# One 128x128 transpose per step in place of eight 64x64 passes, in the triangular inverses of a hybrid mixer kernel

## What is computed

```python
def step(state, inp):
    r_t, w_t, k_t, v_t, kk_t, a_t = inp
    sk = jnp.einsum('bhij,bhj->bhi', state, kk_t)
    state = (state * w_t[:, :, None, :]
             - sk[..., None] * (kk_t * a_t)[:, :, None, :]
             + v_t[..., None] * k_t[:, :, None, :])
    return state, jnp.einsum('bhij,bhj->bhi', state, r_t)
...
_, o = lax.scan(step, s0, xs)
```

## Time and profile before

| | us |
|---|---|
| median of 3 timed runs | 955.85 |
| lowest, highest | 953.41, 956.14 |
| the profiled execution | 953.54 |
| its span from first to last instruction | 951.7 |
| loop of the inverses in it, first L757 to the first L610 behind | 124.02 to 143.63 |

### The profile page before, as it was taken

One profiled execution on the slowest core, in us unless ns is written; L12 is line 12 of the kernel. 1 busy time (PEld: TensorE's weight loads), 2 busy tenths in 40 slices (PEclk: granted clock), 3 DMA queues, 4 the chain that ended last, 5 costly groups with the idle time before them and its releaser, 6 DMA issues.

```text
span 951.7 us, 21560 instructions
## 1 busy us (share of the span) xinstructions
PE 941.5 (99%) x7320; PEld 915.1 (96%) x7320; DVE 748.3 (79%) x1618; ACT 616.7 (65%) x1219; POOL 645.4 (68%) x324
## 2 busy tenths in 40 slices
PE   8999999999999999999999999999999999999997
PEld 7998899999889999999999999999999999999996
DVE  7683574634665889888788888769999999999996
ACT  6874367555557676676899999865555555555553
POOL 4686634488325999999988889966566566567640
PEclk9999999999999999999999999999999999999999
DMA  7463312355654766666555566679999999999981
GB/s 267 145 233 133 133 49 90 110 179 180 223 195 134 250 225 216 217 218 215 199 180 180 182 206 229 217 267 411 408 394 379 403 387 377 408 389 386 386 324 45
DMA packets 67043, 232.36 MB, mean 244 GB/s; under 512 B 8211, under 2 KB 10259, under 8 KB 66860
## 3 DMA queue, kind: packets, MB, share of 16 engines
q1 hardware_dynamic: 52588, 180.51, 53.1%
q0 software_dynamic: 13824, 50.34, 14.0%
q10 hardware_dynamic: 576, 0.82, 0.2%
HBM read 229.67 MB, written 1.06 MB: 242 GB/s over the span
## 4 chain that ended last, share of the span: by engine, by line
PE 97%; DVE 1%; DMA 1%; ACT 0%; issue 0%; ACTq 0%; POOL 0%; DVEq 0%
PE PS L976 21%; PE PS L1047 20%; PE PS L980 12%; PE PS L1051 12%; PE PS L922 3%; PE PS L610 3%; PE PS L614 3%; PE PS L611 3%; PE PS L542 2%; PE PS L534 2%; PE PS L533 2%; PE PS L532 2%; PE PS L933 2%; PE PS L1001 1%; PE PS L1002 1%; PE PS L707 1%
## 5 line engine op out<-in xcount | busy, mean ns | idle before, releaser
L1579 POOL TENSOR_TENSOR lo<-raw,hi 128x1024 fp32r<-128x1024 f32 x191 | 456.7, 2411 | 133.7 <-ACT hi L1129 121.0
L1129 ACT CAST hi<-raw 128x1024 fp32r<-128x1024 f32 x203 | 212.5, 1048 | 56.1 <-DMA raw<-in_u_units 36.6
L976 PE MATMUL PS<-xb,hi 128*128 128x416 f32 x1024 | 219.4, 356 | 0.0
L1047 PE MATMUL PS<-xb,hi 128*128 128x416 f32 x1008 | 213.4, 352 | 0.0
L976 PEld LDWEIGHTS PS<-xb,hi 128*128 128x128 f32 x1024 | 182.5, 189 | 0.9
L1047 PEld LDWEIGHTS PS<-xb,hi 128*128 128x128 f32 x1008 | 179.1, 189 | 1.0
L2274 DVE TENSOR_TENSOR lo<-raw,hi 128x2048 fp32r<-128x2048 f32 x63 | 144.2, 2288 | 7.8 <-ACT hi L1469 7.5
L1469 ACT CAST hi<-raw 128x1024 fp32r<-128x1024 f32 x128 | 134.1, 1047 | 2.4 <-DMA raw<-in_v_units 2.2
L980 PEld LDWEIGHTS PS<-xb,lo 128*128 128x128 f32 x1024 | 133.5, 191 | 1.1 <-POOL lo L1579 0.6
L980 PE MATMUL PS<-xb,lo 128*128 128x208 f32 x1024 | 133.6, 273 | 0.0
L1051 PEld LDWEIGHTS PS<-xb,lo 128*128 128x128 f32 x1008 | 132.4, 191 | 0.7 <-DVE lo L2274 0.5
(11 more groups left out here) (367 smaller groups left out, 1578.4 us busy)
## 6 DMA issues: line engine op xcount, KB each, us to landing
raw<-in_u_units SPq DMA_DIRECT2D x128, 512.0 KB, 3.3
raw<-in_v_units SPq DMA_DIRECT2D x128, 512.0 KB, 6.8
raw<-in_w_in_units SPq DMA_DIRECT2D x43, 512.0 KB, 3.3
raw<-in_w_q_units SPq DMA_DIRECT2D x16, 512.0 KB, 3.2
raw<-in_w_proj_units SPq DMA_DIRECT2D x8, 512.0 KB, 3.3
raw<-in_w_out_units SPq DMA_DIRECT2D x8, 512.0 KB, 3.3
arena<-bias_rows SPq DMA_DIRECT2D x2, 512.0 KB, 5.8
arena<-in_subkeys_t SPq DMA_DIRECT2D x1, 1024.0 KB, 5.5
```

Source lines behind the costliest of these rows:

```text
L976: mm(o[:, 0:2 * TD], hi[:, w, P * k:P * k + P], joined[:, k, 0:2 * TD], start=(k == 0), stop=False, skip_group_check=True)
L1047: return mm(PS[:, V_BANKS[c], 0:2 * TD], hi[:, (U_V + j) % 4, P * c:P * c + P], coef_slot(u + j)[:, 0:2 * TD], start=start, stop=False, sk ...
L1129: nc.scalar.copy(hi[:, j, :], raw[:, j, :]).then_inc(hi_made, 1)
L1579: nc.gpsimd.tensor_tensor(lo[:, w, :], raw[:, w, :], hi[:, w, :].bitcast(F32), ALU.subtract).then_inc(lo_pool, 1)
```

## The change

- **The turn.** In steps 0 to 19 `flip(s)` is one transpose of 128x128 with the whole identity instead of four 64x64 matmuls. It turns the two slots (64 columns each) and both halves at once, so in `W8` the slot is now on the partitions and the half along the free axis. Steps 20 to 23 stay as they were.
- **The first product.** With `W8` laid out so, two of its four 64x64 blocks need the left factor on the other 64 partitions. These crossed factors are made once: two 64x64-weight matmuls of 256 columns with the identity move them into bank 1, behind the scores and ahead of `value_unit(29)`; ScalarE copies them to `S8_crossed`; GpSimd makes `S32_crossed` from that by one masked multiply of 128x256, ahead of its copy of step 4. The four matmuls now use all four quarters of the array, and the rows' halves write two different banks.
- **Banks.** The three products of a step use banks 2q and 2q+1, all eight in all. So the loop starts only when the values are copied out (`vA_sb`), and `flip(1)` waits for the copy of unit 30 (bank 0). `units(31)` waits for `changed(20)` (`x_sb` at 21). Masks and copies read the first product from two banks.
- **The exponentials.** ScalarE's list has two of them ahead of the value copies and three behind, then `gate_copy(30)`; the eight of 256 columns stand at odd steps 1 to 15, the last three of 128 at steps 2, 6 and 10.

```diff
+        def level_at(s):
+            return 2 * (s % 4) + 1 if s < STEPS - 4 else (1, 0, 5, 7)[s % 4]
+        def level_bank(s):
+            return PS[:, level_at(s), 0:P].rearrange("p (a b) -> p a b", b=HD)
+        def p1_banks(s):
+            return PS[:, 2 * (s % 4):2 * (s % 4) + 2, 0:HD] if s < STEPS - 4 else level_bank(s)
...
+            for d in range(2):
+                last = mm(PS[half_rows(1 - d), 1, 0:4 * HD], ident[half_rows(d), half_rows(d)], S8[half_rows(d), 1 - d::2, :],
+                          start=True, stop=True)
+            last.then_inc(sides_ps, 1)
             value_unit(29)
...
             def flip(s):
                 if s >= 4:
                     pe.wait_ge(x_sb, s - 3)
+                if s < STEPS - 4:
+                    nc.tensor.transpose(PS[:, level_at(s), 0:P], WT[:, pairs(s % 4), :].rearrange("p a b -> p (a b)"), ident
+                                        ).then_inc(flip_ps, 1)
+                    return
...
             def first_product(s):
                 pe.wait_ge(flip_sb, s + 1)
-                for m, rows, side in level_blocks(s):
-                    across = mats[rows, 8 * (m // 4) + 4 * (1 - side) + m % 4, 2, half_rows(side)]
-                    inputs = across if s >= STEPS - 4 else (S32 if s >= STEPS - 8 else S8)[rows, m, :]
-                    last = mm(level_out(s, m, side), inputs, W8[rows, m, :], start=True, stop=True)
+                if s < STEPS - 4:
+                    q, wide = s % 4, s >= STEPS - 8
+                    if wide:
+                        pe.wait_ge(sides_sb, 2)
+                    for e, d in ((0, 0), (1, 1), (0, 1), (1, 0)):
+                        if e == d:
+                            left = (S32 if wide else S8)[half_rows(e), 2 * q + e, :]
+                        else:
+                            left = (S32_crossed if wide else S8_crossed)[half_rows(e), q, :]
+                        last = mm(p1_banks(s)[half_rows(d), e, :], left, W8[half_rows(e), 2 * q + d, :], start=True, stop=True)
...
-            pe.wait_ge(xt_dve, 1)
+            pe.wait_ge(sides_sb, 1)
+            pe.wait_ge(vA_sb, 2)
             pe.wait_ge(sc_sb, HEADS)
             for s in range(STEPS):
+                if s == 1:
+                    pe.wait_ge(act_evac, copied(30))
...
+                pe.wait_ge(x_sb, STEPS - 3)
                 units(31 + 3 * n)
...
+                    if lv == 1 and q == 0:
+                        pool.wait_ge(sides_sb, 1)
+                        nc.gpsimd.tensor_tensor(S32_crossed, S8_crossed, con[:, C_NM1 + 3 * HD:C_NM1 + 4 * HD].unsqueeze(1)
+                                                .to_broadcast([P, 4, HD]), ALU.mult).then_inc(sides_sb, 1)
```

More of the change, by code:

```diff
@@ L232, in block_program @@
         nSK = area(R0 + 23040, 1024, 2, 512)
+        S8_crossed, S32_crossed = area(R0 + 23040, 256, 4, HD), area(R0 + 23296, 256, 4, HD)
         ST = area(R0 + 24064, 512, 2, CT, HD)
@@ L748, in level_out @@
             def level_out(s, m, d):
-                return PS[half_rows(d), 4 + s % 4, HD * (m % 2):HD * (m % 2) + HD]
+                return PS[half_rows(d), level_at(s), HD * (m % 2):HD * (m % 2) + HD]
             def flip(s):
@@ L763, in first_product @@
                 pe.wait_ge(flip_sb, s + 1)
-                for m, rows, side in level_blocks(s):
-                    across = mats[rows, 8 * (m // 4) + 4 * (1 - side) + m % 4, 2, half_rows(side)]
-                    inputs = across if s >= STEPS - 4 else (S32 if s >= STEPS - 8 else S8)[rows, m, :]
-                    last = mm(level_out(s, m, side), inputs, W8[rows, m, :], start=True, stop=True)
+                if s < STEPS - 4:
[8 more added lines that the diff above has]
+                        last = mm(p1_banks(s)[half_rows(d), e, :], left, W8[half_rows(e), 2 * q + d, :], start=True, stop=True)
+                else:
+                    for m, rows, side in level_blocks(s):
+                        across = mats[rows, 8 * (m // 4) + 4 * (1 - side) + m % 4, 2, half_rows(side)]
+                        last = mm(level_out(s, m, side), across, W8[rows, m, :], start=True, stop=True)
                 last.then_inc(p1_ps, 1)
@@ L1284, in _ @@
                 hi_ahead(g, 0, 0)
-            act.wait_ge(unit_done, 30)
-            for n in range(NT):
-                nc.scalar.copy(vtokA[:, n, :], PS[:, 2 + n, :]).then_inc(vA_sb, 1)
+            act.wait_ge(sides_ps, 1)
+            nc.scalar.copy(S8_crossed.rearrange("p j t -> p (j t)"), PS[:, 1, 0:4 * HD]).then_inc(sides_sb, 1)
             def exponential(h, n):
@@ L1293, in exponential @@
                                      accum_out=small[:, 16 + 8 * n + h:17 + 8 * n + h]).then_inc(sc_exp, 1)
+            for h in range(2):
+                exponential(h, 0)
+            act.wait_ge(unit_done, 30)
+            for n in range(NT):
+                nc.scalar.copy(vtokA[:, n, :], PS[:, 2 + n, :]).then_inc(vA_sb, 1)
             def first_copied(s):
                 act.wait_ge(p1_ps, s + 1)
-                nc.scalar.copy(P1[:, pairs(s % 4), :], level_bank(s % 4)).then_inc(p1_act, 1)
-            for h in range(4):
+                nc.scalar.copy(P1[:, pairs(s % 4), :], p1_banks(s)).then_inc(p1_act, 1)
+            for h in range(2, 5):
                 exponential(h, 0)
+            gate_copy(30)
             for s in range(STEPS):
                 act.wait_ge(flip_ps, s + 1)
-                nc.scalar.copy(W8[:, pairs(s % 4), :], level_bank(s % 4)).then_inc(flip_sb, 1)
+                nc.scalar.copy(W8[:, pairs(s % 4), :], level_bank(s)).then_inc(flip_sb, 1)
                 if s > STEPS - 8:
                     first_copied(s - 1)
[L1307 to L1312, removed]
+                elif s % 2:
+                    exponential(s // 2, 1)
+                elif s in (2, 6, 10):
+                    exponential(5 + s // 4, 0)
             first_copied(STEPS - 1)
@@ L1888, in masked @@
                 across = con[:, C_LV + HD * lv:C_LV + HD * lv + HD].unsqueeze(1).to_broadcast([P, 2, HD])
-                V.tensor_tensor(P1[:, pairs(q), :], level_bank(q), across, ALU.mult).then_inc(p1_sb, 1)
+                V.tensor_tensor(P1[:, pairs(q), :], p1_banks(s), across, ALU.mult).then_inc(p1_sb, 1)
             def changed(s):
@@ L1895, in changed @@
                 dve.wait_ge(kept, columns_kept(s))
-                w, change = WT[:, pairs(q), :], level_bank(q)
+                w, change = WT[:, pairs(q), :], level_bank(s)
                 old, new = VT[lv % 2][:, pairs(q), :], VT[(lv + 1) % 2][:, pairs(q), :]
```

8 lines of the change are left out of this document (3 added, 5 removed).

## The result

| | before | after |
|---|---|---|
| median of 20 timed runs each, us | 955.39 | 956.52 |
| lowest, highest | 953.41, 956.72 | 955.02, 958.27 |
| the profiled execution | 953.54 | 956.57 |

The ratio of after to before is 1.0013 (95% interval 1.0007 to 1.0019): 1.1 to 1.2 us slower, against a forecast of +1.1. The change is real by this interval and too small to matter: far inside the 0.3% that the prediction called no change.

The account below looks back on a forecast made before the run. TensorE's list was taken to bound the kernel. The terms, 0.63 - 2.5 - 2.3 + 5.3 + 0.1 - 0.1 = +1.1 us, put on the median of 955.85, gave 957.0 us, range 953.0 to 960.5.

Parts of the forecast that it names:

- (a): Ahead of value_unit(29), two matmuls moving the crossed factors add 0.63 us to TensorE's list; bounds 0.48 and 1.1.
- (b): In the loop, 20 turns fall from 0.233 to 0.109 us each: -2.5 us.
- (c): In the loop, 20 first products on four quarters take 0.117 us in place of 0.233: -2.3 us.
- rival A: In the loop, the first product does not run four at a time; at 0.233 us, 959.3 us; chance 0.16.
- (d): In steps 2 to 19, changes of tiling around each transpose cost 0.293 us a step: +5.3 us.
- rival B: In the loop, a lone transpose costs no change of tiling: -1.8 us, 954.1 us; chance 0.22.
- (e): At the loop's start, flip(1) waits for unit 30's copy, with the first W copy queued behind: +0.1 us.
- (f): Around the loop, GpSimd's 0.6 us multiply, two-bank masks, ScalarE's exponentials and unit 31's wait cost nothing.
- (g): In steps 20 to 23, unchanged, changed(16) comes a little earlier against flip(20): -0.1 us.
- Rival C: In the loop, TensorE's clock falls from 2.4 to 1.2 GHz, giving near 967 us; chance 0.03.

Follow-up runs that it names:

- second_turn_beside: The changed kernel with an extra unused transpose right ahead of the turn in steps 1 to 19; ratio 1.0026 to the kernel before.
- second_turn_apart: The changed kernel with an extra unused transpose between first and second product in steps 1 to 19; ratio 1.0078 to the kernel before, four runs.
- sides_only: The kernel before with the two matmuls that move the crossed factors added, their result unused; ratio 0.9997 to the kernel before.
- crossing_by_dma: The changed kernel with the crossed factors moved by two DMAs instead of two matmuls and a copy; ratio 1.0009 to the kernel before.
- pairs: The changed kernel with steps taken in pairs on TensorE, halving the changes of tiling; ratio 1.0020 to the kernel before.
- pairs_dma: The changed kernel with steps in pairs and the crossed factors moved by two DMAs; ratio 1.0012 to the kernel before.
- quarter_turns: The changed kernel with turns 0 to 19 as four 64x64 matmuls on the array's four quarters; ratio 0.9997 to the kernel before.
- quarter_turns_dma: The changed kernel with turns on four quarters, crossed factors by DMA and turn 0 in free banks; 953.70 us, ratio 0.9983 to the kernel before.
- quarter_turns_dma_dense: As quarter_turns_dma, with an exponential in each of steps 1 to 11 of ScalarE's list; ratio 0.9992 to the kernel before.
- dense_exponentials: The changed kernel with an exponential in each of steps 1 to 11 of ScalarE's list; 955.98 us in one execution.

## Why the prediction held

**The bound.** TensorE's list set the end: 1.12 us of it in the trace became 1.13 between the medians. That these agree to 0.01 is luck, for the interval of the ratio is 0.7 to 1.8 us. What carries the claim is all the kernels together. The middle column is what the trace adds to TensorE's list, the moves and the stretch from unit 30 to unit 31; the last is the ratio in us:

| kernel | list, us | time, us |
|---|---|---|
| after | +1.12 | +1.2 (0.7 to 1.8) |
| `second_turn_beside` | +2.99 | +2.5 (1.4 to 3.5) |
| `second_turn_apart` | +8.52 | +7.4 (5.9 to 9.0) |
| `sides_only` | +0.58 | -0.3 (-1.1 to 0.6) |
| `crossing_by_dma` | +0.54 | +0.9 (-0.1 to 1.8) |
| `pairs` | +1.28 | +1.9 (1.0 to 2.8) |
| `pairs_dma` | +0.70 | +1.1 (0.3 to 2.1) |
| `quarter_turns` | +0.60 | -0.3 (-1.1 to 0.6) |
| `quarter_turns_dma` | -1.57 | -1.6 (-2.6 to -0.8) |
| `quarter_turns_dma_dense` | -0.99 | -0.8 (-1.7 to 0.1) |

All lie within their intervals, `sides_only` and `quarter_turns` at the very end of theirs.

**(a), the moves, +0.63**: 0.58, in two kernels. The four passes do overlap, by the price of the two score passes above, though the two row halves write one bank. The 1.1 by the rule of the Trainium skill ("TensorEngine Tiling (Array Packing)", Restrictions and Gotchas, Gotcha 1) did not come about; these halves write different partitions of the bank, and that they overlap there is all that the rows show.

**(b), the turns**: the extra transpose beside the turn added 0.11; 0.109 was forecast.

**(c), the first products**: the second product starts 0.165 behind the first, at most 0.05 of it the dearer first pass behind a change; so the eight passes take the 0.117 that was forecast, not the 0.233 of rival A. `quarter_turns_dma` has the same group without a change beside it, at 0.12.

**(d), the changes**: 0.31 for a visit, 0.293 forecast. The extra transpose apart tests this term almost by itself (tiling and kind of instruction, as said there), and it is the one that decides the case: rival B, that it is nothing, would have made the kernel faster. The split was off where the sum was not. I had put the next turn 0.38 behind the second product; it came 0.33 behind, and the 0.05 sits in the first product, the first group behind the change. The step came out at 0.753 where 0.75 was forecast.

**(e), the start, +0.1**: here errors cancelled. From the first turn to the first product it is +0.07 (125.21 to 126.09 for 124.02 to 124.83). The sum had -0.15 there, because (b) took 0.25 off for turns 0 and 1, which the wait for the copy of unit 30 covers, as (e) itself says. Against this 0.22 stand 0.09 that turn 0 no longer pays for a change of tiling, left out of the sum, and 0.06 in the groups up to turn 3. From unit 30 to turn 3 the terms of the sum come to -0.07 (three turns, two first products, three visits and this 0.1), and the trace has 0.

**(f), at nothing**: GpSimd's multiply is 0.7 long, not 0.6, and hidden; the masks of two banks cost no more (0.20 from the mask to the next operation, where it was 0.24); the looser ScalarE was worth nothing, as `dense_exponentials` says.

**(g), the last steps, -0.1**: -0.12, and -0.10 from turn 19 to turn 20. There TensorE waits for VectorE's change of step 16 in both kernels (turn 20 starts 0.52 behind the second product before and 0.47 now, where 0.23 would do without a wait), so the step cannot be priced from TensorE's passes alone. From turn 19 to unit 31 the terms of the sum come to -0.31, and the trace has -0.22. The kernel before also lost 0.1 between turns 3 and 19 where VectorE was late; with the longer beat this no longer reaches TensorE.

**Rival C** did not come: the clock stayed at 1.00, 2.4 GHz of its two levels, with a transpose in each step. **From the first turn to unit 31** it is 20.24, forecast 20.2.

So the mechanism held, and each part was right to 0.1. That the whole was right to 0.03 is luck: against the sum (1.09 before rounding) the moves came 0.05 lower, the start 0.07 higher, turns 3 to 19 0.08 lower and the rest 0.09 higher. Where my expectations missed was in my own kernels. For `quarter_turns` I had the steps at 0.59 for 0.64, and left out the wait of turn 0 for a bank and the stall at issue. For `pairs` I priced the changes saved, but not that the last levels would have their chain lengthened, and `pairs_dma` inherited this.

**Open.** What makes TensorE wait for its own instructions in the loops of small matmuls is not settled. In both kernels with quarter turns and DMA it came at the same instruction, behind six of the eight passes of turn 17; in `quarter_turns` the long one came inside the first product of step 5. A late load of instructions is a rival that nobody tested: the DMA view, asked in windows of 0.5 us, has a packet of the instruction queue q8 every 4.0 to 4.5 us in the loop before, at distances of 4.5 to 7 in the loop after, with its fewer instructions, and every 3.5 in `quarter_turns`, and none there from 128 to 131, around the stall. That fits TensorE's instructions, but doesn't show that they were late. A first product with both row halves in one bank was not tried, and the first product on two quarters was not isolated.

## What to carry to other kernels

Price an instruction on TensorE by where it stands and not by its passes alone: a cheap full-array transpose among 64x64 matmuls costs 0.11 us of work and 0.3 us of changing there and back, more than the eight small passes that it replaces. Where the small tiles can be spread over all four quarters, this gives nearly the same saving without a change (0.12 for 0.11), at the price of a second bank. And once a loop is shorter, look for what is next (here VectorE at 0.60, ScalarE at 0.65, the bank of the first turn) before counting the gain.

## What the hardware showed that I had not expected

In loops that consist only of 64x64 matmuls at about 0.60 us a step, TensorE once had 0.97 us between two passes of one group with no wait that the profile shows. In the rows of its weight loads (PEld), which show such a gap best, that is 0.83 idle with "issue" as the cause; the same rows have 0.21 at turn 17 of `quarter_turns_dma` and 0.43 at turn 17 of `quarter_turns_dma_dense`. The kernel before has as many instructions in a step, at 0.70, and no such row in its loop.

A DMA within SBUF of 2 x 64 KB, issued as two DMAs from ScalarE's queue (0.66 each there, beside its other work), landed 2.2 us after issue, and saved TensorE 0.58 and ScalarE a copy at no cost that the trace shows.
